# Retention steps one projection block later, selection rounds over three blocks

## The reference, cut to what matters

```python
z = u @ w_in[i]
(aq, ak, av, iq, ik, iw, rq, rk, rv, rg, ga, gb) = jnp.split(z, split_points, axis=-1)
aq, ak, iq, ik = rope(...)                      # each rotated by position
y_a = dsa_attention(aq, ak, av, iq, ik, iw, n_sel)      # attention over the 64 keys with the highest index score
rq, rk = rope(...)
y_r = group_norm_heads(retention(rq, rk, rv), ret_gn[i]) * jax.nn.silu(rg)      # 4 heads
merged = jax.nn.sigmoid(ga) * (y_a @ w_branch_a[i]) + jax.nn.sigmoid(gb) * (y_r @ w_branch_b[i])
h = h + merged @ w_out[i]
```

## The kernel before

| step | TensorE | then |
|---|---|---|
| `ret_scores(h)` | scores from `RK`, `RQ`; waits for rotation 6 | VectorE multiplies by the decay (line 2262) |
| `ret_values(h)` | scores times `RV` | ScalarE copies out (line 1177) |
| `ret_mean(h)` | sum over the head | VectorE subtracts the mean (line 2267), ScalarE squares (line 1515) |
| `ret_var(h)` | sum of the squares | ScalarE takes the root (line 1181), VectorE the reciprocal (line 1701) and scales both halves (line 2273) |

## Time and profile before

### The profile page before, as it was taken

One profiled execution on the slowest core, in us unless ns is written; L12 is line 12 of the kernel. 1 busy time (PEld: TensorE's weight loads), 2 busy tenths in 40 slices (PEclk: granted clock), 3 DMA queues, 4 the chain that ended last, 5 costly groups with the idle time before them and its releaser, 6 DMA issues.

```text
span 1220.2 us, 19104 instructions
## 1 busy us (share of the span) xinstructions
PE 1136.3 (93%) x8002; PEld 966.6 (79%) x8002; DVE 712.8 (58%) x1124; ACT 496.6 (41%) x751; POOL 0.2 (0%) x4
## 2 busy tenths in 40 slices
PE   5898998899999996899999999799999999999986
PEld 3688877645555553899999888698889999999985
DVE  1879686313333325857565677767655676565576
ACT  2674123211111113644344543236864454444353
POOL 0000000000000000000000000000000000000000
PEclk9899868799999998999999989899999999999988
DMA  9845516999999954174544422223235545545410
GB/s 384 346 174 218 207 74 280 364 423 415 410 407 402 403 218 198 60 287 169 207 177 171 155 104 96 104 104 129 96 108 218 192 178 206 196 154 192 147 62 35
DMA packets 38154, 258.39 MB, mean 212 GB/s; under 512 B 4368, under 2 KB 5136, under 8 KB 7856
## 3 DMA queue, kind: packets, MB, share of 16 engines
q1 hardware_dynamic: 36720, 252.90, 53.7%
q10 hardware_dynamic: 1344, 4.21, 0.9%
HBM read 256.05 MB, written 1.05 MB: 211 GB/s over the span
## 4 chain that ended last, share of the span: by engine, by line
PE 82%; DVE 10%; ACT 4%; issue 2%; DMA 2%; DVEq 0%; ACTq 0%; SPq 0%
PE bank L517 81%; DVE wl L1677 1%; ACT wh L1167 1%; DMA csts<-in_cst 1%; DMA raw<-in_f1u 1%; DVE acc L1739 1%; DVE xt L1727 1%; DVE rstd L1701 1%; DVE hl L1744 1%; DVE raw L1716 1%; PE bank L868 0%; DVE arena L1815 0%; ACT arena L1177 0%; DVE arena L1878 0%; DVE arena L2252 0%
## 5 line engine op out<-in xcount | busy, mean ns | idle before, releaser
L517 PE MATMUL bank<-hh,wh 128*128 128x256 f32 (+1 forms) x1256 | 368.4, 293 | 7.6 <-DVE hl L1697 3.8
L517 PE MATMUL bank<-hl,wh 128*128 128x256 f32 (+1 forms) x1256 | 362.7, 289 | 0.0
L517 PE MATMUL bank<-hh,wl 128*128 128x256 f32 (+1 forms) x1256 | 362.3, 288 | 0.0
L1677 DVE TENSOR_TENSOR wl<-raw,wh 128x1024 fp32r<-128x1024 f32 (+2 forms) x236 | 266.8, 1168 | 100.5 <-ACT wh L1167 99.3
L1167 ACT ACTIVATE wh<-raw 128x1024 fp32r<-128x1024 f32 (+2 forms) x236 | 227.0, 1006 | 85.9 <-PE bank L517 77.3
L517 PEld LDWEIGHTS bank<-hh,wh 128*128 128x128 f32 x1256 | 245.5, 195 | 14.7 <-issue 8.4
L517 PEld LDWEIGHTS bank<-hl,wh 128*128 128x128 f32 x1256 | 245.5, 195 | 2.2 <-issue 0.8
L517 PEld LDWEIGHTS bank<-hh,wl 128*128 128x128 f32 x1256 | 245.3, 195 | 1.2
L517 PE MATMUL bank<-yh,wh 128*128 128x256 f32 x512 | 146.6, 286 | 7.7 <-DVE yl L1697 4.9
L517 PE MATMUL bank<-yl,wh 128*128 128x256 f32 x512 | 146.3, 286 | 0.0
L517 PE MATMUL bank<-yh,wl 128*128 128x256 f32 x512 | 146.2, 286 | 0.0
(11 more groups left out here) (243 smaller groups left out, 1368.5 us busy)
## 6 DMA issues: line engine op xcount, KB each, us to landing
raw<-in_gu SPq DMA_DIRECT2D x40, 1024.0 KB, 11.1
arena<-in_gu SPq DMA_DIRECT2D x24, 1024.0 KB, 9.8
raw<-in_gd SPq DMA_DIRECT2D x22, 1024.0 KB, 8.6
raw<-in_w_adt SPq DMA_DIRECT2D x14, 1024.0 KB, 6.2
raw<-in_f1g SPq DMA_DIRECT2D x11, 1024.0 KB, 4.9
raw<-in_f2g SPq DMA_DIRECT2D x11, 1024.0 KB, 4.8
raw<-in_f2u SPq DMA_DIRECT2D x11, 1024.0 KB, 4.8
raw<-in_f2d SPq DMA_DIRECT2D x11, 1024.0 KB, 4.8
```

The lines of the kernel that those rows point to most:

```text
L517: return pe.matmul(o, l, m, start=start, stop=stop, skip_group_check=True)
L1677: v.tensor_tensor(WL[slot_of[U]][:, 0:n], src, WH[slot_of[U]][:, 0:n].bitcast(f32), ALU.subtract).then_inc(S("wl"), 1)
```

## The change

On all three engines the steps of retention move one block back: the scores of head 0 stand behind block `w2rv` 1 instead of `w2rv` 0, and so on, up to the variance of head 3, which now stands behind `w2rg` 0. VectorE's rounds of selection, four before rotation 6 and four behind it, now all stand behind it, as three, three and two, in three blocks. The list of jobs for the banks is moved along with them.

```diff
         put(("rk", 1), ("rot", 5))
-        put(("rv", 0), ("rot", 6), ("rs", 0))
-        put(("rv", 1), ("rw", 0), ("rs", 1))
...
-        put("ak", "av", ("rot", 8), ("rvar", 3), ("rot", 9))
+        put(("rv", 0), ("rot", 6))
+        put(("rv", 1), ("rs", 0))
+        put(("rv", 2), ("rw", 0), ("rs", 1))
...
+        put("ak", "av", ("rot", 8), ("rvar", 2), ("rm", 3), ("rot", 9))
         for h in range(4):
             put(("rg", h))
+            if h == 0:
+                put(("rvar", 3))
             at_jobs(h)
```

TensorE:

```diff
             rotate(6, ("rk", 1), TR[0], 2, 1)
+            lin_tm(("w2rv", 1), [take(pe, ("rv", 1))], 2, H1, L1)
             ret_scores(0)
-            lin_tm(("w2rv", 1), [take(pe, ("rv", 1))], 2, H1, L1)
+            lin_tm(("w2rv", 2), [take(pe, ("rv", 2))], 2, H1, L1)
             ret_values(0)
             ret_scores(1)
-            lin_tm(("w2rv", 2), [take(pe, ("rv", 2))], 2, H1, L1)
+            lin_tm(("w2rv", 3), [take(pe, ("rv", 3))], 2, H1, L1)
             ret_mean(0)
             ret_values(1)
             ret_scores(2)
-            lin_tm(("w2rv", 3), [take(pe, ("rv", 3))], 2, H1, L1)
+            lin_fm(("w2aq", 0), [take(pe, ("aq", 0))], H1, L1)
             ret_var(0)
...
+            ret_var(2)
+            ret_mean(3)
-            ret_var(3)
             rotate(9, "ak", TR[1], 1, 0)
             for h in range(4):
                 lin_fm(("w2rg", h), [take(pe, ("rg", h))], H1, L1)
                 if h == 0:
+                    ret_var(3)
                     evicted(pe, "av")
                 attention(h)
```

VectorE:

```diff
-            pick(0, 4)
             ahead("w2rv", 0)
             rope_rest(6, ("rk", 1), TR[0], 2, 1, RK[:, 2:4, :])
-            pick(4, 8)
+            pick(0, 3)
+            ahead("w2rv", 1)
             ret_scores(0)
-            ahead("w2rv", 1)
+            pick(3, 6)
+            ahead("w2rv", 2)
+            ret_scores(1)
+            pick(6, 8)
             v.tensor_scalar(MB, WK, -3e38, -1e30, ALU.is_gt, ALU.mult).then_inc(S("ix_sel"), 1)
-            ret_scores(1)
-            ahead("w2rv", 2)
+            ahead("w2rv", 3)
             ret_mean(0)
             ret_scores(2)
-            ahead("w2rv", 3)
+            ahead("w2aq", 0)
             ret_var(0)
             ret_mean(1)
             ret_scores(3)
...
             v.wait_ge(*nth("ix_sel", 1))
             for h in range(4):
                 ahead("w2rg", h)
+                if h == 0:
+                    ret_var(3)
```

More of the change, by code:

```diff
@@ L454, in program @@
         put(("rk", 1), ("rot", 5))
-        put(("rv", 0), ("rot", 6), ("rs", 0))
-        put(("rv", 1), ("rw", 0), ("rs", 1))
[L457 to L460, removed]
-        put("ak", "av", ("rot", 8), ("rvar", 3), ("rot", 9))
+        put(("rv", 0), ("rot", 6))
+        put(("rv", 1), ("rs", 0))
+        put(("rv", 2), ("rw", 0), ("rs", 1))
+        put(("rv", 3), ("rm", 0), ("rw", 1), ("rs", 2))
+        put(("aq", 0), ("rvar", 0), ("rm", 1), ("rw", 2), ("rs", 3))
+        put(("aq", 1), ("rot", 7), ("rvar", 1), ("rm", 2), ("rw", 3))
+        put("ak", "av", ("rot", 8), ("rvar", 2), ("rm", 3), ("rot", 9))
         at_jobs = lambda n: put(*([("atv", (n - 3) // 2)] if n >= 3 and n % 2 else []),
@@ L1100, in tensor_program @@
             ret_scores(3)
-            lin_fm(("w2aq", 0), [take(pe, ("aq", 0))], H1, L1)
+            lin_fm(("w2aq", 1), [take(pe, ("aq", 1))], H1, L1)
+            rotate(7, ("aq", 0), TR[1], 2, 0)
             ret_var(1)
@@ L1104, in tensor_program @@
             ret_values(3)
-            lin_fm(("w2aq", 1), [take(pe, ("aq", 1))], H1, L1)
-            rotate(7, ("aq", 0), TR[1], 2, 0)
+            lin_mixed(("w2kv", 0), take(pe, "ak"), take(pe, "av"), 64, H1, L1)
+            rotate(8, ("aq", 1), TR[0], 2, 0)
             ret_var(2)
             ret_mean(3)
-            lin_mixed(("w2kv", 0), take(pe, "ak"), take(pe, "av"), 64, H1, L1)
-            rotate(8, ("aq", 1), TR[0], 2, 0)
-            ret_var(3)
             rotate(9, "ak", TR[1], 1, 0)
@@ L1567, in scalar_program @@
                 copy_out(("rv", i), RV[:, :, i * 256:i * 256 + 256], two(bank(("rv", i))))
-                if i == 1:
+                if i == 2:
                     ret_values(0)
-                elif i == 2:
+                elif i == 3:
                     ret_mean(0)
                     ret_values(1)
[L1573 to L1576, removed]
             ahead("w2aq", 0)
             rope_in(7, ("aq", 0), ("w2aq", 0), TR[1], 2)
+            ret_var(0)
+            ret_mean(1)
+            ret_values(2)
+            ahead("w2aq", 1)
+            rope_in(8, ("aq", 1), ("w2aq", 1), TR[0], 2)
             ret_var(1)
@@ L1581, in scalar_program @@
             ret_values(3)
[L1582 to L1585, removed]
             lin("w2kv", 0)
@@ L2342, in vector_program @@
             ret_scores(3)
-            ahead("w2aq", 0)
+            ahead("w2aq", 1)
+            rope_rest(7, ("aq", 0), TR[1], 2, 0, AQ[:, 0:2, :])
             ret_var(1)
             ret_mean(2)
-            ahead("w2aq", 1)
-            rope_rest(7, ("aq", 0), TR[1], 2, 0, AQ[:, 0:2, :])
+            ahead("w2kv", 0)
+            rope_rest(8, ("aq", 1), TR[0], 2, 0, AQ[:, 2:4, :])
             ret_var(2)
             ret_mean(3)
-            ahead("w2kv", 0)
-            rope_rest(8, ("aq", 1), TR[0], 2, 0, AQ[:, 2:4, :])
-            ret_var(3)
             rope_rest(9, "ak", TR[1], 1, 0, AK.unsqueeze(1))
```

## The result

| | before | changed |
|---|---|---|
| median | 1219.19 us (5 runs, 1215.4 to 1219.84) | 1208.71 us (5 runs, 1208.49 to 1212.7) |
| span of the profiled execution | 1220.2 us | 1210.5 us |
| TensorE waits, 756 to 850 | 8.4 us | 2.2 us |

The ratio is 0.9935, with a 95% interval of 0.9917 to 0.9953: 7.9 us faster. In a second set of runs, on one chip with three of the experiments, it was 0.9943 (0.9928 to 0.9957). The forecast was 8.0 us and 1208.4. The two medians lie 10.5 apart and the ratio, taken over all executions, says 7.9: two more executions of the kernel before lifted its median from 1216.37, on which the forecast stood, to 1219.19. With single executions of one kernel up to 4.4 us apart, that 1208.4 was hit within 0.3 is luck; what tests the forecast is the stage in the trace, 8.3 against 8.0.

A forecast was written before the change was run, and what follows sets the result against it. TensorE's idle wait and slow clock were taken as the bound: -8.36 - 2.29 - 0.86 + 3.5 = -8.0 us, from a 1216.37 median to 1208.4, range 1204.8 to 1213.2.

The forecast's parts named there:

- The stall's cause and its price: Before head 0's scores, TensorE waits 8.36 us for a rotation behind VectorE's selection; removing wait and slow clock gains 10.65.
- The slow clock behind it, 2.29: Scores and block w2rv 1 after the idle wait run mostly at 1.2 GHz, costing 2.29 us.
- The walk of VectorE's queue: VectorE's new order through the retention blocks brings no new TensorE waits; tightest margins 1.7, 1.5 and 1.2 us.
- The rival of the returning stall: VectorE slips 3.5 us in retention; TensorE waits 2.3 and the clock takes 2.3, giving 1213.0; chance 0.16.
- Head 3's variance, the price: Behind w2rg 0, root, reciprocal and scaling become uncovered; first product starts 4.25 us after the block instead of 0.74.
- the rival in which attention absorbs the late start: In the attention stage the late first product costs nothing; only wait and clock count, giving 1205.7 us; chance 0.10.
- Attention's new wait: TensorE waits about 1.9 us before the first transposes of probabilities, then about 1 once or twice more.
- That the clock would not fall: At attention's new wait, slow clock was taken as 0; if it fell, at most 1.3 us would show.

The follow-up runs named there:

- selection alone: Kernel before with only VectorE's selection rounds moved behind rotation 6, retention steps left in place; ratio 0.9940 to the kernel before.
- 8, 0, 0: Changed kernel with all eight selection rounds directly behind rotation 6 instead of three, three, two; ratio 1.0032 to the kernel before.
- 4, 4, 0: Changed kernel with selection rounds laid out four, four, none instead of three, three, two; ratio 0.9970 to the kernel before.
- shift alone: Changed kernel with selection rounds put back, four before and four behind rotation 6, keeping the one-block shift; ratio 1.0015 to the kernel before.

## Why the prediction was right, step by step

**The stall's cause and its price.** Right. Scores and block 1 together were to end at 769.44 instead of 780.09, 10.65 earlier; they end at 769.12, 10.97 earlier. The term was 0.3 too small, mostly because I let block 1 begin at the rotation product's shown end, 762.98. Its first matmul is issued at 762.40, beside the product's tail, and it reaches the scores at 768.55 and not at 768.82. This 0.3 is all by which the stage beat the forecast. The kernel with the selection alone shows that this wait was the selection's.

**The slow clock behind it, 2.29.** Right here: the changed kernel has 1.00 from 762 to 822. As a rule it was too narrow. The kernel with 8, 0, 0 paid 2.9 behind nearly the same wait.

**The walk of VectorE's queue.** Right, and the margins were measured twice. Forecast 1.7, 1.5 and 1.2; in the trace 1.81, 1.76 and 1.6 (squares end at 789.67, asked for at 791.25). And the rounds as 4, 4, 0 gave waits of about 0.3 and 1.81 where 0.2 and 2.2 were expected from them. The rival of the returning stall didn't come about, but lies one or two rounds away.

**Head 3's variance, the price.** Right. w2rg 0 was to end at 821.9 and ends at 821.58; the product was to start at 826.15, and starts at 825.82; leaving the work out gives 2.63 back. So the rival in which attention absorbs the late start is out as well. ScalarE's timeline of the changed kernel shows the gate's table behind the root:

```profile
822.72 0.47 ACT L1183 ACTIVATE rstd<-bank,small 128x256 f32<-128x256 f32 x1 [1.50 <-PE bank L519]
823.22 1.28 ACT L1179 ACT_TABLE_LOAD   x1
824.51 0.60 ACT L1179 ACTIVATE arena<-bank 128x512 f32<-128x512 f32 x1
```

The activation starts right behind the load, at 824.51, and is covered by VectorE. The Trainium skill's 2.66 us for a switch (ScalarE: Activation LUTs, What ACT_TABLE_LOAD costs) for load and drain would, as an estimate from that figure, have set it near 825.9 and the product near 826.5; the trace doesn't agree with that, and the measurement decides.

**Attention's new wait.** Forecast 1.9, found 1.61. The prediction's own terms give 831.7 - 830.0 = 1.7, so 0.2 of the difference is a slip in that sum. About 1 was forecast once or twice more, and 0.63 and 0.59 were found. That the clock would not fall was right for the changed kernel in both its profiles, but it was luck in part: in the kernel with 8, 0, 0 it fell at the same wait, and the 1.3 that I gave as the most that could show is what showed.

**What the prediction did not ask.** It took the change as one thing. The experiments split it: the selection brings all of the gain, the shift by a block brings nothing of its own (0.5 slower alone, 0.6 slower as part of the change, each by one trace's stage). The shift cures a wait of 1.67 at its start. At its end it pays 3.5, less the 0.86 of TensorE's work that leaves the stretch in front of w2rg 0.

## What to carry to other kernels

When an engine's optional work stands in front of what another engine waits for, move that work alone first, and count the wait that is left before shifting a whole chain of steps. A chain shifted by one block comes out one block later at its far end; ask what covered its last link until now, and whether half a block, or only the first link, would do. Read the margin of each producer against the moment when its result is asked for: here margins between 1.6 and 1.8 told within 0.4 the wait that two more rounds in front of a decay product would bring.

## What the runs showed of the hardware

**Waits of the same length don't have the same price.** The clocks here are those granted to TensorE in the 4 us behind a wait; before each the clock was at 1.00, the 2.4 GHz level.

| wait of TensorE | clock stayed at 1.00 | clock lower |
|---|---|---|
| 1.61, before the first transposes | 4 traces | 1 trace (0.64) |
| 1.67, before the merge | 7 traces | none |
| 1.67 (selection alone) and 1.81 (rounds 4, 4, 0), in the stage | both | none |
| 1.82, before the merge | 1 trace | 2 traces (0.63, 0.64) |
| 1.80, near 104 | 3 traces | 5 traces (0.65, 0.66) |
| 2.06, near 27 | 3 traces | 7 traces (0.57 to 0.64) |
| 2.3, near 698 | none | 10 traces (0.57 to 0.65) |
| 2.46 and 2.63, shift alone | none | both (0.59, 0.64) |
| 2.8 to 3.1, near 488 | 3 traces | 7 traces (0.58 to 0.66) |

So between 1.6 and 3.1 the length alone doesn't say whether the clock falls, and what else decides it isn't shown. A wait in this range costs its length, and where the clock fell inside the stage 1.3 to 1.7 more. The Trainium skill (TensorE: Matmul & The Clock Gate, Why this matters for your kernels) warns of idle gaps between bursts of matmuls; the traces agree for the waits in the right column, not for those in the middle one.

**Most of the scatter between executions lies ahead of this stage, and goes with the granted clock.** The rotation product comes anywhere from 753.4 to 764.1, while the stretch behind the stage differs by 3.3 (308.0 to 311.3). ScalarE's second root of the first block (timeline of ScalarE below, first for the selection alone, then for the shift alone) comes anywhere from 201.2 to 208.6, though all ten traced kernels run the same instructions up to there:

```profile
201.34 0.47 ACT L1181 ACTIVATE rstd<-bank,small 128x256 f32<-128x256 f32 x1 [1.17 <-PE bank L517]
```
```profile
208.57 0.47 ACT L1183 ACTIVATE rstd<-bank,small 128x256 f32<-128x256 f32 x1 [1.17 <-PE bank L519]
```

The windows of the same two, in the same order:

```profile
0.00:100.00 100.00, 78.54 (x532) 63.94 (x532) 64.37 (x109) 55.48 (x99) 0.20 (x4) 0.97 0.76 300
100.00:200.00 100.00, 94.78 (x578) 84.02 (x576) 74.30 (x132) 29.31 (x48) 0.00 (x0) 0.83 0.46 174
```
```profile
0.00:100.00 100.00, 79.70 (x525) 64.68 (x526) 61.70 (x104) 54.77 (x98) 0.20 (x4) 0.93 0.77 300
100.00:200.00 100.00, 94.00 (x533) 83.17 (x533) 71.97 (x125) 27.64 (x42) 0.00 (x0) 0.78 0.39 144
```

Over the first 200 us the mean clock is 0.90 in the two traces whose root comes at 201.2 and 201.3, 0.88 or 0.89 in the four from 204.3 to 204.9, 0.87 in the two at 206.7 and 207.3, and 0.85 in the two at 208.4 and 208.6: the lower the clock, the later the root. The waits near 27 and 104 of the table are among the places where the traces part. That is 7 us against the 2 us between two of the variants, and why the stage length was read beside the medians. Why the clock fell in one execution and not in the next was not looked into.
